# Two accumulating stores in flight in a mixture-of-experts stage, with a reordered list of experts

## What is computed

```
scores = sigmoid(t @ w_router); biased = scores + router_bias
top_group = argmax over groups of (sum of the two best biased scores in the group)
top_e = the two best experts inside that group
gates = scores[top_e] / sum(scores[top_e])
act = silu(t @ w_gate[e]) * (t @ w_up[e]) * gate
out = sum over the two experts of act @ w_down[e]
```

## Time and profile before

| what | value |
|---|---|
| median of 3 runs | 1334.93 us (1334.38 to 1335.98) |
| the profiled execution | 1336.83 us |
| its span, first to last instruction | 1335.0 us |
| mean granted TensorE clock | 0.986 |
| busy: PE, VectorE, ScalarE, GpSimd | 94%, 44%, 25%, 17% |
| chain that ended last | PE 77%, DMA 12%, DVE 6%, issue 2% |
| in it, DMA xrows<-big,info | 11% |
| moved by DMA | 266.83 MB, 198 GB/s over the span |

### The profile page before, as it was taken

The page is one execution under the profiler, slowest core; times in us unless marked ns, Lnnn a source line. Parts: engine busy times, 40 slices in busy tenths (PEclk is TensorE's granted clock), DMA queues, the critical chain, the costliest instruction groups (busy, mean ns, idle before and its releaser), DMA issues.

```text
span 1335.0 us, 20021 instructions
## 1 busy us (share of the span) xinstructions
PE 1256.9 (94%) x7823; PEld 721.2 (54%) x7823; DVE 591.0 (44%) x1510; ACT 332.1 (25%) x783; POOL 229.3 (17%) x296
## 2 busy tenths in 40 slices
PE   4999999999999899998989999999999998999995
PEld 3665466666645554444444455555785455444442
DVE  4221266566545754434352000001884566444446
ACT  4121355445422300000032000001983330000002
POOL 6220500100100011223220100004221001211230
PEclk8899999999999999999989999999999999999999
DMA  9512411221664479999671373135325435999966
GB/s 377 186 39 74 180 65 65 88 106 65 237 263 154 143 292 377 392 379 393 158 257 67 112 252 127 64 127 174 104 73 187 198 112 228 387 380 379 352 164 219
DMA packets 45165, 266.83 MB, mean 200 GB/s; under 512 B 6948, under 2 KB 13428, under 8 KB 31232
## 3 DMA queue, kind: packets, MB, share of 16 engines
q1 hardware_dynamic: 22672, 192.85, 36.8%
q0 software_dynamic: 16640, 51.73, 14.0%
q10 hardware_dynamic: 5760, 20.97, 4.0%
HBM read 230.19 MB, written 33.76 MB: 198 GB/s over the span
## 4 chain that ended last, share of the span: by engine, by line
PE 77%; DMA 12%; DVE 6%; issue 2%; ACT 2%; ACTq 0%; DVEq 0%; SPq 0%; POOLq 0%
PE PS L901 13%; DMA xrows<-big,info 11%; PE PS L1284 10%; PE PS L1124 10%; PE PS L1174 10%; PE PS L1191 5%; PE PS L1041 5%; PE PS L766 4%; PE PS L772 4%; PE PS L788 3%; PE PS L1081 3%; PE PS L1346 2%; PE PS L988 2%; DVE big L1692 2%; PE PS L1309 1%
## 5 line engine op out<-in xcount | busy, mean ns | idle before, releaser
L1124 PE MATMUL PS<-weights,ht 128*128 128x512 f32 x320 | 142.3, 596 | 1.7 <-DVE ht L1692 1.0
L1284 PE MATMUL PS<-ht,weights 128*128 128x128 f32 (+1 forms) x512 | 140.2, 434 | 1.5 <-PE PS L788 0.9
L901 PE MATMUL PS<-weights,ht 128*128 128x336 f32 (+1 forms) x320 | 119.6, 533 | 2.6 <-ACT ht L1471 1.6
L1174 PE MATMUL PS<-big 128*128 128x512 f32 x256 | 115.4, 603 | 3.5 <-DVE big L2145 3.5
L1284 PEld LDWEIGHTS PS<-ht,weights 128*128 128x128 f32 x512 | 77.8, 191 | 64.1 <-issue 64.1
L766 PEld LDWEIGHTS PS<-const,big 128*128 128x128 f32 (+2 forms) x611 | 74.8, 144 | 64.1 <-issue 36.2
L766 PE MATMUL PS<-const,big 128*128 128x128 f32 (+2 forms) x611 | 90.5, 285 | 19.3 <-DMA big<-hrows,info 5.5
L1599 ACT ACTIVATE big<-PS 128x256 f32<-128x256 f32 x34 | 13.1, 385 | 336.0 <-PE PS L1174 336.0
L1124 PEld LDWEIGHTS PS<-weights,ht 128*128 128x128 f32 x320 | 59.0, 190 | 69.1 <-issue 69.1
L901 PEld LDWEIGHTS PS<-weights,ht 128*128 128x128 f32 x320 | 61.7, 195 | 55.6 <-issue 42.1
L1692 DVE TENSOR_TENSOR big<-PS,big 128x512 f32<-128x512 f32 (+1 forms) x70 | 44.2, 672 | 98.0 <-DMA xrows<-big,info 49.9
(11 more groups left out here) (255 smaller groups left out, 1793.1 us busy)
## 6 DMA issues: line engine op xcount, KB each, us to landing
weights<-in_ada SPq DMA_DIRECT2D x22, 2048.0 KB, 8.7
big<-in_gu SPq DMA_DIRECT2D x16, 2048.0 KB, 18.4
weights<-in_gu SPq DMA_DIRECT2D x12, 2048.0 KB, 21.6
rows<-in_down SPq DMA_DIRECT2D x18, 1024.0 KB, 11.7
weights<-in_down SPq DMA_DIRECT2D x16, 1024.0 KB, 16.1
ht<-in_gu SPq DMA_DIRECT2D x6, 2048.0 KB, 22.0
weights<-in_qkv SPq DMA_DIRECT2D x6, 2048.0 KB, 11.5
weights<-in_wo SPq DMA_DIRECT2D x4, 2048.0 KB, 8.3
```

Of the source, the lines that this page charges most:

```text
L901: ins = pe.matmul(bank(4 + u % 2, n), lhs(k), rhs(k), start=(k == 0), stop=(k == ks - 1))
L1124: ins = pe.matmul(bank(4 + j), OT[:, k, t * P:(t + 1) * P], w[j][:, k, :], start=(k == 0), stop=(k == KD - 1))
L1174: ins = pe.matmul(bank(0), gatT[:, k, :], w[:, k, :], start=(k == 0), stop=(k == KD - 1))
L1284: ins = pe.matmul(bank(bb, n1 - n0), w[:, k, m * P:(m + 1) * P], hT[:, k, n0:n1], start=(k == 0), stop=(k == KD - 1))
```

## The change

- The fixed tiles take the experts in the order `EXPERT`, in which neighbours are of different groups. The wait for the previous accumulating store before an `add_static` is gone. What remains is that a buffer `yb` is rewritten only once the store from it, two tiles back, has landed. Odd tiles send their empty rows to a second block of 128 spare rows (`odd_at`), which is zeroed at the start, two more small stores.
- The transposes of tile 15 move into the last fixed slot, those of tile 17 into the trip, and the gathers of tiles 17 and 18 are issued ahead of the accumulating stores of tiles 14 and 15. The last down product goes to the same banks as the others.
- `release` and TensorE's waits for its own products are gone. SP waits for the product semaphore itself (`products_done`).
- The 2 MB `ada` chunk for layer 1 is issued behind the loop's loads.

```diff
@@ -55,6 +55,8 @@
 MAXT = E + XTILES
 TILES = MAXT + 2
 STAT = E - 1
+EXPERT = (0, 4, 12, 8, 1, 5, 13, 9, 2, 6, 11, 7, 3, 10, 14)
+ODD = slice(4, 11)
...
@@ -385,6 +387,23 @@
             n = LOADS[g].index((what, l, j))
             return SLOTS_[g][n], w_rank(g, n)
 
+        def products_done(what, l, j):
+
+            if what == "ada":
+                return m_mm, l * 12 + (FRONT.index(j) if l * 12 + j < 4 else j) + 1
+            if what == "ukv":
+                return k_mm, H // 2
+            if what == "uq":
+                return g_mm, AT_MM["uq"] + (j + 1) * 10
+            if what == "qkv" and j < 4:
+                return qk_mm, 4 * (QK.index(4 * j) // 4 + 1)
+            return g_mm, AT_MM["vproj" if what == "qkv" else what] + 2 * NT - 1 + j % 2
+
+        def last_in(slot, g, n):
+
+            every = [(i, x) for y in range(2) for i, x in zip(SLOTS_[y], LOADS[y])]
+            return [x for i, x in every[:n + g * len(SLOTS_[0])] if i == slot][-1]
+
         def w_wait(eng, what, l=0, j=0):
 
             slot, r = w_slot(what, l, j)
@@ -428,10 +447,10 @@
             sp.dma_start(const[:, :], a["const"][:, 0:NCONST]).then_inc(s_const, 16)
 
             def static_load(g, n):
-                if w_rank(g, n):
-                    sp.wait_ge(w_used[SLOTS_[g][n]], w_rank(g, n))
                 src = source(*LOADS[g][n])
                 slot = SLOTS_[g][n]
+                if w_rank(g, n):
+                    sp.wait_ge(*products_done(*last_in(slot, g, n)))
                 if slot == 3:
                     half = src.shape[1] // 2
                     sp.dma_start(R[:, 0:half], src[:, 0:half]).then_inc(w_in[slot], 16)
...
@@ -508,9 +527,6 @@
                     load_gu(n)
                     sp.wait_ge(e_dn[l], n - 4)
                     load_dn(n - 1)
-                    if l == 0 and n == 8:
-                        sp.wait_ge(n_st, stored("f0"))
-                        static_load(1, 0)
                 sp.wait_ge(rr_tab, l + 1)
                 trips = sp.value_load(rtx[0:1, 31:32], min_val=1, max_val=5)
                 with sp.Fori(0, trips) as i:
@@ -524,7 +540,9 @@
                         sp.wait_ge(e_gu[l], free + (j + 1))
                         sp.dma_start(GU[j], a["gu"][l][bass.ds(gu, 1)]).then_inc(e_gw[l][j], 16)
                 if l == 0:
+                    sp.wait_ge(n_st, stored("f0"))
                     sp.wait_ge(e_gu[l], STAT - 1)
+                    static_load(1, 0)
                     static_load(1, 1)
                 sp.wait_ge(e_dn[l], trips * 2 + (STAT - 2))
                 last = sp.value_load(rtx[0:1, bass.ds(trips * 2 + (STAT - 1), 1)], min_val=0, max_val=E - 1)
...
@@ -716,15 +735,14 @@
                 def add_static(n):
 
                     pool.wait_ge(e_yd[l], n + 1)
-                    if n:
-                        pool.wait_ge(e_ys[l][(n - 1) % 2], 16 * ((n - 1) // 2 + 1))
-                    add_rows(tok_at[:, n:n + 1], n % 2)
+                    at, e = (odd_at, EXPERT[n] - ODD.start) if n % 2 else (tok_at, EXPERT[n])
+                    add_rows(at[:, e:e + 1], n % 2)
 
                 for n in range(3, STAT + 2):
                     if n == STAT:
                         pool.wait_ge(e_tab[l], 1)
                     pool.wait_ge(e_tr[l], n - 1)
-                    rows_of(tok_at[:, n:n + 1] if n < STAT else last_token(n - STAT + 3), n % 2)
+                    rows_of(tok_at[:, EXPERT[n]:EXPERT[n] + 1] if n < STAT else last_token(n - STAT + 3), n % 2)
                     if n >= 4:
                         add_static(n - 4)
...
@@ -734,8 +752,11 @@
                 pool.wait_ge(rr_tab, l + 1)
                 trips = pool.value_load(rtx[0:1, 31:32], min_val=1, max_val=5)
                 with pool.Fori(0, trips) as i:
+                    pool.wait_ge(e_tr[l], i * 2 + (STAT + 1))
+                    pool.nop().then_inc(e_gate, 1)
+                    rows_of(last_token(5), 1)
                     for par in range(2):
...
                     for j in range(2):
 
                         pool.wait_ge(e_yd[l], i * 2 + (STAT + j))
@@ -751,17 +775,9 @@
                         pool.nop().then_inc(e_gate, 1)
                         add_rows(last_token(j), j)
 
-                        pool.wait_ge(e_tr[l], i * 2 + (STAT + 1 + j))
-                        pool.nop().then_inc(e_gate, 1)
-                        rows_of(last_token(3 + j), 1 - j)
-
 
         @block.tensor
         def _(pe):
-            def release(what, l=0, j=0):
-                if w_used[w_slot(what, l, j)[0]] is not None:
-                    pe.nop().then_inc(w_used[w_slot(what, l, j)[0]], 1)
-
...
@@ -788,8 +804,6 @@
                         ins = pe.matmul(PS[32 * g:32 * g + 2, ada_out_at(i):ada_out_at(i) + P], condT[:, 2 * k:2 * k + 2],
                                         w[:, k, g * P:(g + 1) * P], start=(k == 0), stop=(k == KD - 1))
                 ins.then_inc(m_mm, 1)
-                pe.wait_ge(m_mm, i + 1)
-                release("ada", l, j)
 
             def mod_transpose(i):
 
...
-                        rows_T((n + 1) % 2, 16 * (n // 2 + 1))
+                    rows_T((n + 1) % 2, 16 * (n // 2 + 1))
                     if n:
                         b = (n - 1) % 4
                         down(b, d_in[b], 16 * (DNS[b] * l + (n - 1) // 4 + 1), n, n - 1 or None)
@@ -1204,19 +1204,19 @@
                 pe.wait_ge(rr_tab, l + 1)
                 trips = pe.value_load(rtx[0:1, 31:32], min_val=1, max_val=5)
                 with pe.Fori(0, trips) as i:
-                    rows_T(1, i * 16 + 16 * 8)
                     gateup(0, e_gw[l][0], i * 16 + 16, i * 2 + (STAT + 1))
                     rows_T(0, i * 16 + 16 * 8)
                     down(2, e_dw[l][0], i * 16 + 16, i * 2 + STAT, i * 2 + (STAT - 1))
                     acts_T(i * 2 + (STAT + 1))
                     gateup(1, e_gw[l][1], i * 16 + 16, i * 2 + (STAT + 2),
                            lambda: down(3, e_dw[l][1], i * 16 + 16, i * 2 + (STAT + 1), i * 2 + STAT))
+                    rows_T(1, i * 16 + 16 * 9)
                     acts_T(i * 2 + (STAT + 2))
-                down(2, e_dw[l][0], trips * 16 + 16, trips * 2 + STAT, None, 3)
+                down(2, e_dw[l][0], trips * 16 + 16, trips * 2 + STAT, trips * 2 + (STAT - 1))
                 pe.wait_ge(e_dn[l], trips * 2 + STAT)
 
-                pe.wait_ge(e_ta[l], trips * 2 + STAT)
-                pe.wait_ge(e_td[l], trips * 2 + STAT)
+                pe.wait_ge(e_ta[l], trips * 2 + (STAT + 1))
+                pe.wait_ge(e_td[l], trips * 2 + (STAT + 1))
                 if l == 0:
                     ada(1, 4)
                 pe.wait_ge(e_yd[l], trips * 2 + STAT)
...
@@ -1939,6 +1930,7 @@
                 toks, gates = bank(6, TILES), bank(6, TILES, TILES)
                 dve.tensor_scalar(tok_at.bitcast(U32), toks[:, 0:STAT], spare, 2048.0, ALU.min, ALU.add).then_inc(rr_info, 1)
                 link(dve.tensor_copy(gate_at, gates[:, 0:STAT]))
+                dve.tensor_scalar(odd_at.bitcast(U32), toks[:, ODD], const[:, C_SPARE_ODD:C_SPARE_ODD + 1], 2048.0, ALU.min, ALU.add)
                 for at in (last_tok[:, 2:15], last[:, 0]):
                     dve.tensor_scalar(at.bitcast(U32), toks[:, STAT - 1:], spare, 2048.0, ALU.min, ALU.add)
                 dve.tensor_copy(last[:, 1], gates[:, STAT - 1:]).then_inc(e_tab[l], 1)
```

More of the change, by code:

```diff
@@ L466, in load_gu @@
                     b = n % 5
-                    sp.dma_start(GU[b], a["gu"][l][n]).then_inc(u_in[b], 16)
+                    sp.dma_start(GU[b], a["gu"][l][EXPERT[n]]).then_inc(u_in[b], 16)
                 def load_dn(n):
                     b = n % 4
-                    sp.dma_start(DN[b], a["down"][l][n]).then_inc(d_in[b], 16)
+                    sp.dma_start(DN[b], a["down"][l][EXPERT[n]]).then_inc(d_in[b], 16)
                 def static_done(slot):
-                    return sum(x.count(slot) for x in SLOTS_[:l + 1])
+                    return products_done(*last_in(slot, l, len(LOADS[l])))
                 if l == 1:
@@ L1181, in acts_T, with down @@
                     ins.then_inc(e_at[l], 1)
-                def down(b, w_in_, w_ready, tiles, free, out=1):
+                def down(b, w_in_, w_ready, tiles, free):
                     pe.wait_ge(w_in_, w_ready)
@@ L1190, in down @@
                         for k in range(2):
-                            ins = pe.matmul(bank(out + n), actT[:, k, :], w[:, k, n * 512:(n + 1) * 512], start=(k == 0), stop=(k == 1))
+                            ins = pe.matmul(bank(1 + n), actT[:, k, :], w[:, k, n * 512:(n + 1) * 512], start=(k == 0), stop=(k == 1))
                     ins.then_inc(e_dn[l], 1)
```

78 lines of the change are left out of this document (30 added, 48 removed).

## The result

The changed kernel takes **1314.26 us** (median of 6 runs, 1311.17 to 1315.46); the kernel before, beside it on the same chip, takes 1333.64. The ratio is 0.986, with a 95% interval from 0.9837 to 0.9882, so it is 19.4 us faster. The forecast was 1320.0, with a range from 1314 to 1331. The profiled execution has a span of 1313.6 us (1335.0 before) at a mean granted clock of 0.989 (0.986). PE is busy for 95% of it, and the chain that ended last is 85% PE and 5% DMA (77% and 12% before).

What follows compares the result with a forecast made beforehand. It took late gathered rows, behind serial stores, to stall PE in layer 0. 10.1 + 1.4 + 1.1 - 1.0 + 3.8 - 0.4 = 15.0 us took the profiled 1336.83 to 1321.8; less 1.9 for the median, 1320.0, range 1314 to 1331.

Steps and rivals of the forecast that it cites:

- the row queue: Expert stages: two stores in flight let the DMA queue of gathered rows keep TensorE's pace, 11.40 us a tile.
- What bounds the kernel: Layer 0's fixed tiles: stores waiting for earlier stores delay gathers, so PE waits for rows; store 8 is 15.1 us late.
- 10.1 us forecast for layer 0's tiles: Layer 0, gateup 1 to gateup 15: 170.2 us falls to 160.1, tile 15's moved transposes included; gain 10.1 us.
- The rival of the row queue that is no faster: Layer 0's tiles: engines are full, a second store only waits, rows stay late; about 1330.5 us, chance 0.14.
- The slower rival: Expert stages: two accumulating stores slow each other, rows cost half more a MB; 1343.5 us, chance 0.04.
- The room of 16.6 us: Gate and up loads, issued 45.6 us before use, land in 29.0, leaving 16.6 us free to give to rows.
- The trip and layer 1: Layer 0's trip after gateup 15 gains 1.4 us net; layer 1's tiles gain 1.4, less 0.3 in its trip: 1.1.
- The 0.3 for tile 17's transposes: Trip of each layer: part of VectorE's copy delays the last down product; cost 0.3 us, bounds 0 and 1.4.
- The ends: End of each expert stage: gather 17 ahead of store 14 delays it; cost 0.5 us a layer, together -1.0.
- TensorE's waits for itself: Five groups of waits for its own products, 15 places: all their idle time is gained, 3.8 us, bounds 0 and 6.2.
- The small parts: Head of each expert stage: VectorE makes one more table, costing 0.4 us for both; zeroing stores and late chunk cost nothing.

Runs made afterwards that it cites:

- e1: Changed kernel with GpSimd again waiting for the previous accumulating store to land before each fixed tile's store; 1323.93 us.
- e2: Changed kernel with the 2 MB ada chunk issued in the middle of layer 0's fixed tiles again; 1314.00 us.
- e3: Kernel before, with only the ada chunk moved behind the loop's loads; 1334.28 us.
- h1: Changed kernel with tile 15's transposes and copies back at the top of the loop and none of tile 17's in the trip; 1317.59 us.
- h2: Changed kernel with two needless 2 MB loads beside layer 0's fixed tiles, at tiles 5 and 8; 1320.76 us.
- f1: Changed kernel with TensorE's waits for its own products and the empty counting instruction behind each put back; 1320.23 us.
- e4: Changed kernel with TensorE's waits for its own products put back, without the empty counting instruction; 1318.72 us.
- h4_after_again: The changed kernel run once more with no edit, beside the later experiments on one chip; 1313.66 us.

## Why the prediction was right

The main step, the row queue, held and is shown. The total held narrowly: 1314.26 lies 0.3 above the lower end of the range and below the forecast's own range of 1316 to 1323. The gain was 19.4 us for 15.0.

**What bounds the kernel, and the row queue** (10.1 us forecast for layer 0's tiles): measured 10.6, slots of 11.40 us, and e1, e2 and e3 show that it is the stores, with 1.5 us for tile 15's transposes by h1. It is a little more than forecast because the first slot lost its slow clock (7.11 for 7.56); e3, with the stores of before, has lost it too, so this 0.5 us is chance. The rival of the row queue that is no faster fell, and with it, as an argument against a second store, the rule of the Trainium skill (DMA: Bandwidth & Descriptors, Issuing engines are not separate DMA queues) that all queues end on the same engines. The rule and the gain hold together: at a share of 1.02 and 1.03 the engines were full before and after, but the holes of q0 had gone to weights that were not yet needed (q1's 72.1% of the time fell to 68.0%). The slower rival fell by the same rows: the price of a MB of rows did not change.

**The room of 16.6 us** was right as a reason why PE would not stop among the tiles (10 us more cost 1.0 there) and wrong as something free: h2 paid 3.9 to 6.1 us at the end. It is wrong for tile 15 as well, whose load goes out 33.4 us before its use and not 45.6. The text had nothing on the end of the stage in this step. It did the sum no harm, since the change adds no load.

**The trip and layer 1**: 1.4 and 1.1 forecast. T1 to T15 in layer 1 gained 1.46, as 1.4 said. The 0.3 for tile 17's transposes in each trip was not seen: in layer 1 the last down product starts 24.66 us after gateup 15 in both kernels. From gateup 15 to the `ada` product of layer 0 the trip fell from 30.12 to 28.71 us. That is the forecast's 1.4, but by luck, since a wait of 0.35 us for the last down product took the place of the 0.3.

**The ends** (-1.0): the mechanism was there, store 14 at 18.5 us after gateup 15. From T15 on, trip and end together gained 1.4 us in layer 0 and lost 0.5 in layer 1. The forecast for these stretches was +0.9 (1.4 for the trip, -0.5 for the end) and -0.8 (-0.3 and -0.5). In layer 1, kernels with the changed trip lose 0.1 to 0.7. The end itself cost nothing in layer 0, where `ada` product to B is 62.71 us before and after. In the second profile of the same kernel it even gained 2.3: gather 17 landed in 10.35 us for 11.28, and the reload went out 1.5 us sooner after gateup 15.

**TensorE's waits for itself** (3.8): this term was mis-sized. A to T0, B to C and C to T0 gained 0.78 + 3.93 + 0.60 = 5.3 us. A further 1.2 us lie before A, from the first `uq` product on. Kernel before and changed kernel:

```profile
89.89 4.11 PE L901 MATMUL PS<-weights,rows 128*128 128x384 f32 x12
```

```profile
87.70 4.04 PE L915 MATMUL PS<-weights,rows 128*128 128x384 f32 x12
```

From there to A it is 68.31 and 67.15 us. Every kernel with the pair of wait and empty instruction has 68.31 (before, e3, f1), e4 with the wait alone 67.80, and every kernel without a wait 67.15 or 67.16. So the waits are worth 6.5 us, and 6.8 without the 0.3 us of low clock in the router, which is more than the 6.2 that the text had as upper bound. Two things failed. The text took only five of the groups and left out others in the same stretches, such as the waits behind the output projections (L865, 0.6 us). And the idle time in the rows is not the whole price: the twenty waits shown from the first `uq` product on sum to 5.1 us. In f1 the ten between B and C sum to 3.0 us, while the stretch is 4.06 longer. By an estimate from these two numbers a wait takes away another 0.1 us by which products in a stream overlap.

**The small parts** (-0.4): T0 to T1 shows -0.1 in each layer; the rest was not seen apart.

The sum of the measured parts is 10.6 + 1.4 - 0.1 + 1.5 - 0.1 - 0.5 + 6.5 = 19.3 us (19.2 before rounding), against 15.0. The profiled pair differs by 21.4; the other 2.2 lie before the first `uq` product. Most of it is the clock in the first products of `win`. Before and changed kernel, from their chains of waits:

```profile
40.58 24.53 PE PS L901 x80
```

```profile
40.24 22.84 PE PS L915 x80
```

This is no part of the change: h4_after_again and e2, without waits, have 24.53 too, and f1, with all of them, 22.84.

So of the 5.7 us between the forecast 1320.0 and 1314.26, 4.2 are in the terms, and 1.3 in the median of the kernel before, which was 1334.93 when the forecast was made and is 1333.64 beside the changed kernel. That the rest is small is luck as well, since medians of the kernel before lie between 1331.6 and 1336.1.

## What to carry to other kernels

A DMA share of 1.0 doesn't say that every queue is late: look at which one has holes, and at what moves in them and is early. Keep accumulating stores apart by the order of the work and not by a wait, and the slower queue can run at the pace of the engine. Bytes that a full stage hides are paid at its end, so look there for what a moved or added load costs; and where an engine waits for its own products only to tell another engine so, let the other one wait.

## What the hardware showed unexpectedly

- An empty instruction that only counts a semaphore costs TensorE nothing in a stream (153.99 us with and without), 0.24 us behind a wait. The wait alone costs 0.16 us at an `ada` product and 0.2 on average, and leaves no idle time in the profile there.
- The queue of small row transfers gives way last. With four needless loads, from 530 to 640 us, `big` and `weights` loads of gate and up landed in 43.0 and 48.1 us (25.9 and 29.9 in h4_after_again), and stores in 15.0 (12.3), still issued 11.40 us apart until PE was late.
- Neither a DMA share of 1.0 nor the number of stores in flight set the price of rows: 3.8 us a MB with one and with two.
- One and the same program differs by 2.2 us between two profiles in a stretch of 90 us (T15 to B) and by 1.5 before A (kernels alike up to there by up to 4), while its other stretches repeat to 0.4 us, most to 0.05. Comparing landmarks tells a cause of 0.5 us which medians with a scatter of 2 us don't.
- In the router TensorE's clock falls to its lower level in some kernels and not in others (granted 0.50, 0.69 and 1.00 over the same work), worth up to 1.8 us from one kernel to another.
